# Expert tail with two groups at a time and one sum per chunk, and decay rows of a forgetting head moved up in VectorE's order

## What is computed

```python
xn = rmsnorm(h, attn_norm_g)
# forgetting head: decay c_q - c_k is added to the logits
logits = q_blk @ k_ctx.T * HEAD_DIM ** -0.5 + c_q[..., :, None] - c_k[..., None, :]
h = h + concat([fox * gate_f, sb]) @ w_out
hn = rmsnorm(h, ffn_norm_g)
# experts: 8 heads x top 16 of 128 x 128 keys per token
h = h + sum_e g_e * gelu(u[idx_e] . hn) * v[idx_e]
```

## Time and profile before

| | |
|---|---|
| median of three runs | 3444.09 us (3443.67 to 3444.48) |
| profiled execution, its own time | 3442.3 us |
| its span | 3440.6 us |
| TensorE busy | 3356.8 us, 98% |
| VectorE busy | 2254.7 us, 66% |
| ScalarE busy | 1083.4 us, 31% |
| GpSimd busy | 766.1 us, 22% |
| mean granted TensorE clock | 0.992 |

### The profile page before, as it was taken

How to read it: one execution, slowest core, us unless ns; L and a number is a source line. 1 busy time by engine, 2 the same in 40 slices (tenths; PEclk the granted TensorE clock), 3 DMA queues, 4 the chain that set the end, 5 groups by cost and what they waited for, 6 DMA issues and landing times.

```text
span 3440.6 us, 42143 instructions
## 1 busy us (share of the span) xinstructions
PE 3356.8 (98%) x16745; PEld 2955.0 (86%) x16745; DVE 2254.7 (66%) x3081; ACT 1083.4 (31%) x1102; POOL 766.1 (22%) x375
## 2 busy tenths in 40 slices
PE   7999999998989999999999999999999999999999
PEld 5777778887878899999989998998998998988887
DVE  4464541112027887867488788788878887888776
ACT  5232324443231134444322222222222322223232
POOL 4333333333433310000122222122122122120000
PEclk9999999999999999999999999999999999999999
DMA  3222222223222234454788898888898888887765
GB/s 135 86 73 75 84 74 74 86 73 124 96 86 87 97 118 174 165 187 177 259 324 308 304 335 303 309 325 306 308 330 303 310 321 307 322 320 275 243 235 181
DMA packets 153932, 713.50 MB, mean 207 GB/s; under 512 B 12032, under 2 KB 72448, under 8 KB 73984
## 3 DMA queue, kind: packets, MB, share of 16 engines
q1 hardware_dynamic: 116992, 444.12, 36.4%
q0 software_dynamic: 36864, 268.45, 21.2%
HBM read 674.51 MB, written 38.01 MB: 207 GB/s over the span
## 4 chain that ended last, share of the span: by engine, by line
PE 65%; issue 24%; POOL 6%; DVE 3%; DMA 1%; ACT 1%; POOLq 0%; DVEq 0%; ACTq 0%
PE bank L349 11%; PE bank L351 11%; PE bank L350 11%; PE bank L373 9%; PE bank L372 9%; PE bank L374 9%; POOL wl L335 5%; PE bank L1577 2%; DMA gate_scratch<-arena 1%; DVE wl L1209 1%; DVE acc L1298 0%; ACT wh L329 0%; DMA raw<-in_v 0%; PE bank L1541 0%; DVE acc L389 0%
## 5 line engine op out<-in xcount | busy, mean ns | idle before, releaser
L349 PE MATMUL bank<-xh,wh 128*128 128x384 f32 (+1 forms) x3184 | 1148.4, 361 | 9.1 <-DVE wl L1209 5.1
L351 PE MATMUL bank<-xh,wl 128*128 128x384 f32 (+1 forms) x3184 | 1130.1, 355 | 0.0
L350 PE MATMUL bank<-xl,wh 128*128 128x384 f32 (+1 forms) x3184 | 1129.3, 355 | 0.0
L329 ACT ACTIVATE wh<-raw 128x2048 fp32r<-128x2048 f32 x345 | 659.7, 1912 | 931.1 <-PE bank L374 704.7
L1209 DVE TENSOR_TENSOR wl<-raw,wh 128x2048 fp32r<-128x2048 f32 x253 | 579.2, 2289 | 345.6 <-ACT wh L329 345.3
L349 PEld LDWEIGHTS bank<-xh,wh 128*128 128x128 f32 x3184 | 600.9, 189 | 54.8 <-DVE wl L1209 5.4
L350 PEld LDWEIGHTS bank<-xl,wh 128*128 128x128 f32 x3184 | 600.9, 189 | 45.3 <-issue 1.9
L351 PEld LDWEIGHTS bank<-xh,wl 128*128 128x128 f32 x3184 | 599.8, 188 | 45.5
L335 POOL TENSOR_TENSOR wl<-raw,wh 128x2048 fp32r<-128x2048 f32 x92 | 425.4, 4625 | 785.2 <-ACT wh L329 785.2
L640 POOL DMA_INDIRECT arena<-in_u_rows,g_idx x128 | 158.9, 1241 | 1141.6 <-DVE acc L1298 468.2
L374 PE MATMUL bank<-wh,gl 128*128 128x512 f32 x1008 | 392.7, 390 | 0.0
(11 more groups left out here) (182 smaller groups left out, 2660.9 us busy)
## 6 DMA issues: line engine op xcount, KB each, us to landing
raw<-in_u SPq DMA_DIRECT2D x128, 1024.0 KB, 4.8
raw<-in_v SPq DMA_DIRECT2D x128, 1024.0 KB, 5.2
raw<-in_w_in SPq DMA_DIRECT2D x57, 1024.0 KB, 4.7
gate_scratch<-arena SPq DMA_DIRECT2D x12, 2048.0 KB, 7.2
arena<-gate_scratch SPq DMA_DIRECT2D x32, 768.0 KB, 7.6
raw<-in_w_out SPq DMA_DIRECT2D x16, 1024.0 KB, 4.7
raw<-in_w_pq SPq DMA_DIRECT2D x16, 1024.0 KB, 4.7
act_scratch<-arena SPq DMA_DIRECT2D x44, 192.0 KB, 1.9
```

The source lines that it names most:

```text
L329: nc.scalar.activation(wh[s][:], raw[s][:], ACT.Copy).then_inc(hi_done, 1)
L349: nc.tensor.matmul(dst, w_h[:, c], xh[:, c, 0:width], start=(c == 0), stop=False)
L350: nc.tensor.matmul(dst, w_h[:, c], xl[:, c, 0:width], start=False, stop=False)
L351: last = nc.tensor.matmul(dst, w_l[:, c], xh[:, c, 0:width], start=False, stop=(c == KC - 1))
```

## The change

The tail's groups are taken as sets: group 0 alone, then five pairs (`TAIL_SETS`). TensorE multiplies both groups of a pair for one chunk before it goes to the next, and they add up in PSUM, so that VectorE adds each chunk once for each set: 24 times three banks where it was 44 times three. The groups' weights lie in `xh` and `xl` at eight places for each set (`tail_weights`), so the buffers of two sets alternate. TensorE's tail is unrolled. The orders of SyncE, ScalarE and VectorE are written anew. The slots of the tail go by set: 1, 3, 2, 2, 2, 2 instead of 2 and then ten times 1. The first weights of a pair's second group are needed one unit behind those of its first. In the forgetting heads, `decay_dve(h)` of heads 1 to 7 stands behind the head's first `copy_out`.

```diff
@@ -87,12 +87,20 @@
 ROW_BUFS = 3
 
 TURN_AHEAD = 5
+TAIL_SETS = [(0,)] + [(_r, _r + 1) for _r in range(1, LAG, 2)]
+SET_START = [sum(CH * len(_q) for _q in TAIL_SETS[:_n]) for _n in range(len(TAIL_SETS))]
+TAIL_UNITS = [(_n, _c, _r) for _n, _q in enumerate(TAIL_SETS) for _c in range(CH) for _r in _q]
+assert LAG % 2 == 1 and len(TAIL_UNITS) == GRP * LAG
...
+SLOT_COUNTS += [1] + [_rest // (len(TAIL_SETS) - 1) + (_n < _rest % (len(TAIL_SETS) - 1))
+                      for _n in range(len(TAIL_SETS) - 1)]
 GROUP_SLOTS = []
-for _r in range(NGRP):
+for _n in SLOT_COUNTS:
     _s = GROUP_SLOTS[-1].stop if GROUP_SLOTS else 0
-    _n = (GM - _r % 2) if _r < NMAIN else 1 + (_r == NMAIN)
     GROUP_SLOTS.append(range(_s, _s + _n))
-assert GROUP_SLOTS[-1].stop == SLOTS
+assert GROUP_SLOTS[-1].stop == SLOTS and max(SLOT_COUNTS) <= GM
 
 V_ORDER = [0, *range(LAG, NGRP), *range(1, LAG)]
 
...
             return 2 * GROUP_SLOTS[r].start + second * len(GROUP_SLOTS[r]) + j
 
+        def tail_weights(buf, r, j):
+
+            q = (r + 1) // 2
+            return buf[:, 8 * (q % 2) + 4 * (r - TAIL_SETS[q][0]) + j, 0:TD]
+
         def wait_from(eng, s, n):
 
...
@@ -566,18 +579,28 @@
                 main_sp(g, g * 4 + CH * (LAG - 1), None, False)
             main_sp(NMAIN - 1, CH * V_ORDER[NMAIN - 1], CH * V_ORDER[NMAIN], True)
 
-            for r in range(LAG):
-                if r < LAG - 1:
-                    sp.wait_ge(w_lo, 4 * (NMAIN + r + 1))
-                    load_acts(NMAIN + r + 1)
-                    load_gates(V_ORDER[NMAIN + r + 1])
-                for c in range(CH):
-                    n = CH * r + c + 2
-                    if n < CH * LAG:
-                        load(sp, N_TAIL + n, v[CH * V_ORDER[NMAIN + n // CH] + n % CH])
+            def load_group(r):
+
+                sp.wait_ge(w_lo, 4 * (NMAIN + r))
+                load_acts(NMAIN + r)
+                load_gates(V_ORDER[NMAIN + r])
+
+            def load_tail(n):
+
+                if n < GRP * LAG:
+                    _, c, r = TAIL_UNITS[n]
+                    load(sp, N_TAIL + n, v[CH * V_ORDER[NMAIN + r] + c])
+
+            for q, members in enumerate(TAIL_SETS):
+                for i in range(CH * len(members)):
+                    if i == 0 and 2 * q + 1 < LAG:
+                        load_group(2 * q + 1)
+                    if i == (3 if q == 0 else 4) and 2 * q + 2 < LAG:
+                        load_group(2 * q + 2)
+                    load_tail(SET_START[q] + i + 2)
             out_t = out.rearrange("(b p) d -> p b d", p=P)
             for c in range(CH):
-                sp.wait_ge(chunk_out, 24 + 3 * (4 * (NGRP - 1) + c + 1))
...
@@ -866,13 +889,14 @@
                 act.wait_ge(gather_used, turn_of(r, 0, True))
                 nc.scalar.activation(dots[:, 0:ns], dots[:, 0:ns], ACT.Gelu).then_inc(dots_act, 1)
 
-            def tail_w_act(i, r, first=False):
-
-                if not first:
-                    act.wait_ge(unit_done, i * 8 + (N_TAIL + 4 * (r - 1)))
+            def tail_w_act(r):
+
+                q = (r + 1) // 2
+                if q:
+                    act.wait_ge(unit_done, N_TAIL + SET_START[q - 1])
                 for j in range(GRP):
-                    act.wait_ge(w_gated, i * 8 + (NMAIN + r) * 4 + j + 1)
-                    nc.scalar.activation(xh[:, 4 * (r % 2) + j, 0:TD], h_grp[:, j * TD:(j + 1) * TD],
+                    act.wait_ge(w_gated, (NMAIN + r) * 4 + j + 1)
+                    nc.scalar.activation(tail_weights(xh, r, j), h_grp[:, j * TD:(j + 1) * TD],
                                          ACT.Copy).then_inc(w_hi, 1)
 
             def main_act(g, last):
...
-            for r in range(LAG):
-                for c in range(CH):
-                    if r < LAG - 1 or c < CH - 1:
-                        split_hi(act, N_TAIL + 4 * r + c + 1)
-                    if c == 0 and r < LAG - 1:
-                        tail_w_act(0, r + 1)
-                    if c == 2:
-                        dots_gelu(NMAIN + r)
+            for q, members in enumerate(TAIL_SETS):
+                for i in range(CH * len(members)):
+                    n = SET_START[q] + i
+                    if n + 1 < GRP * LAG:
+                        split_hi(act, N_TAIL + n + 1)
+                    if i == (0 if q == 0 else 1) and 2 * q + 1 < LAG:
+                        tail_w_act(2 * q + 1)
+                    if i == (3 if q == 0 else 4) and 2 * q + 2 < LAG:
+                        tail_w_act(2 * q + 2)
+                    if i == (3 if q == 0 else 6):
+                        dots_gelu(NMAIN + q)
 
 
         @block.vector
...
@@ -990,6 +1017,7 @@
                                             ALU.add).then_inc(freed[0], 1)
                 copy_out(1, q_raw, h, 4)
                 if p is not None:
+                    decay_dve(h)
                     vtok_dve(p)
                 copy_out(2, k_raw, h, 4)
                 if p is not None:
@@ -1009,7 +1037,7 @@
                     dve.wait_ge(csum_done, 2)
                     nc.vector.tensor_tensor(csum, csum, csum_hi.bitcast(F32), ALU.subtract).then_inc(csum_done, 1)
                     dve.wait_ge(csum_done, 3)
-                decay_dve(h)
+                    decay_dve(h)
                 rms_dve(h)
 
             fox_dve(0, None)
...
@@ -1351,39 +1378,76 @@
                 main_lo(g, 8)
                 add_row(g, 3)
...
-            tail_chunk(LAG - 1, 3)
+            def tail_chunk(q, c):
+
+                n = len(TAIL_SETS[q])
+                add_chunk(dve, N_TAIL + SET_START[q] + n * c + n - 1, 12 + 8 * (NMAIN + q) + 2 * c, c,
+                          DENSE_BANKS[c % 2])
+
+            def tail_lo(q, i):
+                if SET_START[q] + i < GRP * LAG:
+                    lo(N_TAIL + SET_START[q] + i)
+
+            main_chunk(NMAIN - 1, 3)
+            tail_lo(0, 1)
+            gate_mult(NMAIN + 1)
+            for j in range(4, len(GROUP_SLOTS[NMAIN - 1])):
+                add_row(NMAIN - 1, j)
+            tail_chunk(0, 0)
+            tail_lo(0, 2)
+            tail_rest(1)
+            tail_chunk(0, 1)
+            tail_lo(0, 3)
+            dot(NMAIN, 0)
+            tail_chunk(0, 2)
+            tail_lo(0, 4)
+            gate_mult(NMAIN + 2)
+            coefs(NMAIN)
+            tail_rest(2)
+
+            for q in range(1, len(TAIL_SETS)):
+                s = NMAIN + q
+                ns = len(GROUP_SLOTS[s])
+                before = range(min(2, len(GROUP_SLOTS[s - 1])) if q > 1 else 0, len(GROUP_SLOTS[s - 1]))
+                more = q < len(TAIL_SETS) - 1
+                tail_chunk(q - 1, 3)
+                tail_lo(q, 1)
+                for j in before[:2]:
+                    add_row(s - 1, j)
+                tail_lo(q, 2)
+                if more:
+                    gate_mult(NMAIN + 2 * q + 1)
+                for j in before[2:]:
+                    add_row(s - 1, j)
+                dot(s, 0)
+                tail_chunk(q, 0)
+                tail_lo(q, 3)
+                if more:
+                    tail_rest(2 * q + 1)
+                tail_lo(q, 4)
+                for j in range(1, min(3, ns)):
+                    dot(s, j)
+                tail_chunk(q, 1)
+                tail_lo(q, 5)
+                if more:
+                    gate_mult(NMAIN + 2 * q + 2)
+                tail_lo(q, 6)
+                if more:
+                    tail_rest(2 * q + 2)
+                if ns > 3:
+                    dot(s, 3)
+                tail_chunk(q, 2)
+                tail_lo(q, 7)
+                for j in range(4, ns):
+                    dot(s, j)
+                coefs(s)
+                tail_lo(q, 8)
+                for j in range(min(2, ns)):
+                    add_row(s, j)
+            last = NMAIN + len(TAIL_SETS) - 1
+            for j in range(2, len(GROUP_SLOTS[last])):
+                add_row(last, j)
+            tail_chunk(len(TAIL_SETS) - 1, 3)
 
 
         @block.tensor
@@ -1620,17 +1684,14 @@
                     v_chunk(N_MAIN + GRP + c, c, c, lambda e: gh[:, e * TD:(e + 1) * TD],
                             lambda e: gl[:, e * TD:(e + 1) * TD], g, 8, 4)
 
-            def tail_pe(i, r):
-                pe.wait_ge(w_lo, i * 8 + 4 * (NMAIN + r + 1))
-                w = 4 * (r % 2)
-                for c in range(CH):
-                    v_chunk(N_TAIL + 4 * r + c, 4 * (NMAIN + r) + c, c, lambda e: xh[:, w + e, 0:TD],
-                            lambda e: xl[:, w + e, 0:TD], i, 8, 8)
-
-            with pe.Fori(0, LAG // 2) as i:
-                tail_pe(i, 0)
-                tail_pe(i, 1)
-            tail_pe(LAG // 2, 0)
+            for n, (q, c, r) in enumerate(TAIL_UNITS):
+                members = TAIL_SETS[q]
+                if c == 0:
+                    pe.wait_ge(w_lo, 4 * (NMAIN + r + 1))
+                d = 4 * (NMAIN + q) + c
+                chunk_unit(pe, N_TAIL + n, DENSE_BANKS[c % 2], r == members[0], r == members[-1],
```

(2 more changed lines are left out.)

41 lines of the change are left out of this document (6 added, 35 removed).

## The result

The changed kernel takes 3421.39 us (median of four runs, 3419.08 to 3424.15) where the kernel before takes 3443.88 beside it: ratio 0.9936 [0.9919, 0.9953], 22.5 us less. Two repeats on other occasions gave 3424.22 against 3444.80 (0.9939 [0.9925, 0.9952]) and 3423.77 against 3441.08 (0.9946 [0.9932, 0.9959]), 20.6 and 17.3 less. The forecast was 3432.6 us, 11.5 less, in a range from 3425 to 3441. One of the nine runs of the kernel before that stood beside e3_head1, e5_nogather, e8_swap and e7_behind took 3558.22 us at a granted clock of 0.905, and the ratios and the medians here leave it out.

A forecast was written before the change was run, and what follows sets the result against it. The prediction took TensorE's time, and its waits, to bound the kernel. Heads -15.3 and tail +3.8 gave -11.5 us, so 3430.8 from the profiled 3442.3, plus 1.8 for the median: 3432.6 us, range 3425 to 3441.

The forecast's parts named there:

- What bounds the kernel: Whole kernel: TensorE, busy 98%, sets the time, so only its waits count.
- Decay rows, the gain: Heads: reciprocals start earlier without the decay rows ahead, removing seven logits waits of 1.94 us, 13.6 us gained.
- Decay rows, the new place: Heads, behind the first copy: the decay rows fit into VectorE's idle time even if held by GpSimd, price 0.
- Clock in head 1: Head 1, 145 to 149 us: the fall to a lower clock goes with the idle time before it, -1.7 us.
- Tail, what is removed: Tail: three TensorE waits go, -1.9 us; fewer VectorE sums and the unrolled loop give 0.
- Tail, what is added: Tail: group loads landing in 11.5 us make TensorE wait 4.0 us for unit 6, plus 1.7 us of clock.
- Sum: Whole kernel: heads -15.3 and tail +3.8, together -11.5 us.
- (a): Tail: group loads are quick (8.6 us), no new wait, 3427 us; chance 0.20.
- (b): Tail: group loads are slow (13.5 us or more), +9.7 us in the tail, 3438.5 us; chance 0.16.
- (c): Heads: reciprocals wait for GpSimd after all, so the heads give 10 instead of 13.6, 3436 us; chance 0.08.
- (d): Tail: every group load from the third on meets gathers and nine stop TensorE, some 3470 us; chance 0.05.
- (e): Heads: moved decay rows do nothing because another operation holds the logits, +3.8 alone, 3448 us; chance 0.06.

The follow-up runs named there:

- e3_head1: Changed kernel with head 1's decay rows back at their old place, heads 2 to 7 at the new one; 3426.59 us, ratio 0.9952.
- e5_nogather: Kernel before without the tail's 12 slots, so no row gathers, dot products or v rows there; 3442.01 us (one run).
- e8_swap: Kernel before with each group load of the tail queued ahead of the unit's load instead of behind it; 3443.26 us (one run).
- e7_behind: Changed kernel with gathers beside the loads of groups 2 and 3, and group 3's load behind unit 6's; 3425.96 us, ratio 0.9951.
- e2_tail: Changed kernel with the decay rows back at their old place, so only the tail's change remains; 3441.92 us, ratio 0.9991.
- e6_unroll: Kernel before with TensorE's tail unrolled and nothing else; 3442.60 us, ratio 0.9997.
- e10_slack: Changed kernel with group 3's load put behind unit 6's load in the queue; 3423.88 us, ratio 0.9948.
- e9_twice: Changed kernel with the gates of group 3 loaded twice and unit 6's load behind that; 3434.48 us, ratio 0.9974.
- e1_decay: Kernel before with only the decay rows of heads 1 to 7 moved behind the head's first copy; 3426.91 us, ratio 0.9947.

## Why the prediction was half right

- **What bounds the kernel**: right. The time is TensorE's, and its waits are what the change moved.
- **Decay rows, the gain** (13.6): the mechanism was right in each link. The reciprocals start 1.39 us behind the gate product, where I had 1.3, take 6.56 beside GpSimd's subtraction and are not held. The logits follow the last product by 0.23. The size was short: a head gains 2.2 us, not 1.94. I had 198.85 as the time at which TensorE is ready and wrote 2.3 us of cover, and still priced the step by the listed idle time. The difference of starts, 200.94 - 198.85 = 2.09, was in the same rows. 15.4 instead of 13.6.
- **Decay rows, the new place** (0): right, with the 4.3 us of being held that were forecast as possible, and 3.74 us left.
- **Clock in head 1** (-1.7): right. 1.6 to 1.7 by the rows, and e3_head1 shows that the fall comes back with the idle time. That it was head 1 and no other is not explained.
- **Tail, what is removed** (-1.9, sums 0, loop 0): right. The tail of e2_tail is 2.2 shorter, the waits and 0.3 for restarts, and e6_unroll gives 0.
- **Tail, what is added** (+4.0 + 1.7): this is the step that failed. The wait for unit 6 did not come, because the 11.5 us put in for the gates' landing was wrong. The chain's other links held to 0.6 us. Taking off the 17.0 us gained in the heads, I had group 2's gates issued at 3073.2 (they were at 3072.94), and TensorE ready for unit 6 at 3103.5 (its first product stands at 3103.52). Only the low parts of group 2 start 2.72 us behind the product's start (3083.42 to 3086.14) where I had 2.1, since VectorE waits 0.68 for ScalarE there. The 11.5 was taken between 8.6 and 13.5 as if a gather 6 us behind still cost part of what a near one costs. It cost nothing: its first packets flow at 3083.5, when the gates have landed. The gather must meet gates that are still held up by a unit's load. Group 2's load had its unit's load 2.3 us ahead (9.9), group 3's had no load close ahead (8.2). With these two numbers the chain has unit 6 ready at 3119.9 against 3120.5, a slack of 0.6, and the trace has 0.1. So the 4.0 and the 1.7 fall away. Two smaller slips in the prediction change nothing: with 13.5 for both its chain waits 8.0 and not 8.2, and nine of the ten loads took 13 us or more, not eight.
- **Sum**: -11.5, less the 5.7 that didn't come, less 1.7 in the heads, less 0.3 for restarts in the tail and 0.4 elsewhere: -19.6, the difference of the spans. The medians say -17 to -22.5.
- **Rivals**: (a), quick group loads, is what happened, and I had given it 0.20. Its 3427 lacked the 1.7 of the heads. It said "no wait" with unit 6 ready at 3120.4 against 3120.5, and the trace has just that slack. That is luck: it had 8.6 for both loads, and the two were 9.9 and 8.2. The row that it took 8.6 from, group 1 of before, lands in 7.9 to 11.5 in other traces. (b), (c), (d) and (e) did not happen: gates of 9.9 at most from group 2 on, reciprocals not held, no wait that repeats, and 17.9 us from the decay rows alone.
- **The range**: its low end, 3425, was rival (a) and "a little below". The heads' 13.6 had no bound of its own, so 1.7 us of undercounted heads and a few us of run to run difference were enough to leave it.

## What to carry to other kernels

Price a removed wait by the starts of the instructions around it, not by the listed idle time: here 1.94 listed were 2.2 gained, seven times. Measure over a stretch that repeats: the heads' logits agree within 0.1 us from trace to trace, the spans only within some 5. A duration of a transfer in a trace belongs to what flows beside it. Before taking a value between two rows, look at what was issued ahead in the same queue, and at when the packets of the other queues flow and not when they were issued, because two causes may only act together. When a computed slack is near zero, say so: the queue's order can be changed for free, as in e10_slack, and a load late by 7.7 us cost 9.4 in e9_twice.

## What the hardware did that I had not expected

- Gates with a unit's load ahead and a gather behind landed in 13.5 us, with the unit's load alone in 8.9, with the gather alone in 6.9. Half-KB packets moved 0.08 MB in 2 us beside 8 KB packets, and 0.30 MB in 1 us alone.
- Beside a group's loads a gather's packets began 4.4 us behind its issue (before, 3163.13) or 4.9 (e8_swap, 3164.07), which is why a gather 2 us behind a load may do no harm. With no group load under way they began 1.7 us behind it (before, 3154.66). What makes the difference stays open.
- Of seven equal idle times (1.94 us) one or two brought the clock to its lower level. It was head 1's in before, e2_tail, e3_head1, e5_nogather and e8_swap (PEclk 0.66 to 0.69 from 145 to 150 us), heads 1 and 2 in e6_unroll, and none in the changed kernel and e1_decay, which don't have these waits. After the single idle time of 7.54 us it was 0.50 for the next 2 us of work.
